# The last modulation group on VectorE inside the down projection, instead of TensorE in the up projection

## The reference, cut to what matters

```python
for l in range(DEPTH_2):
    sh_l, sc_l, g_l = jnp.split(jax.nn.silu(c) @ w_mod[l] + b_mod[l], 3, axis=-1)
    sh_c, sc_c, g_c = jnp.split(jax.nn.silu(c_ctx) @ w_mod[l] + b_mod[l], 3, axis=-1)
    hl = xl * (1.0 + sc_l[:, None, :]) + sh_l[:, None, :]
    hc = xc * (1.0 + sc_c) + sh_c
    ...
```

## Time and profile before

| | us |
|---|---|
| median of three runs | 3048.57 |
| lowest and highest run | 3047.79, 3052.81 |
| the profiled execution | 3046.77 |
| its span, first to last instruction | 3045.0 |
| TensorE busy with matmuls | 2971.8 |
| VectorE busy | 1683.7 |
| ScalarE busy | 1352.8 |
| up projection | about 796 to 1326 |
| down projection | about 1326 to 1574 |

### The profile page before, as it was taken

How to read it: one execution, slowest core, us unless ns; L and a number is a source line. 1 busy time by engine, 2 the same in 40 slices (tenths; PEclk the granted TensorE clock), 3 DMA queues, 4 the chain that set the end, 5 groups by cost and what they waited for, 6 DMA issues and landing times.

```text
span 3045.0 us, 48466 instructions
## 1 busy us (share of the span) xinstructions
PE 2971.8 (98%) x19848; PEld 2526.0 (83%) x19848; DVE 1683.7 (55%) x2625; ACT 1352.8 (44%) x2084; POOL 43.8 (1%) x84
## 2 busy tenths in 40 slices
PE   8999999999899999999999999999999999999997
PEld 7888876898588888788888887788888998889996
DVE  6666666443766666664464325554562575357754
ACT  5333334434455555454452224544442472255543
POOL 1000000000000000000000000000000000000000
PEclk9999999999999999999999999999999999999998
DMA  7665655446765666745553222222232442234442
GB/s 266 223 222 210 220 195 214 140 165 263 276 233 210 228 230 257 279 157 183 185 182 102 97 93 83 76 87 83 83 142 97 166 168 96 97 129 145 153 155 108
DMA packets 73799, 510.03 MB, mean 167 GB/s; under 512 B 8325, under 2 KB 8465, under 8 KB 19601
## 3 DMA queue, kind: packets, MB, share of 16 engines
q1 hardware_dynamic: 63504, 435.74, 40.6%
q0 software_dynamic: 10112, 71.60, 5.9%
HBM read 503.10 MB, written 6.55 MB: 167 GB/s over the span
## 4 chain that ended last, share of the span: by engine, by line
PE 93%; DVE 5%; ACT 1%; DMA 1%; issue 0%; SPq 0%; ACTq 0%; DVEq 0%
PE bank L773 22%; PE bank L717 16%; PE bank L716 8%; PE bank L1496 6%; PE bank L1498 6%; PE bank L1497 6%; PE bank L916 3%; PE bank L917 2%; PE bank L918 2%; PE bank L948 2%; PE bank L1056 2%; PE bank L814 2%; PE bank L815 1%; PE bank L816 1%; PE bank L1123 1%; PE bank L1521 1%
## 5 line engine op out<-in xcount | busy, mean ns | idle before, releaser
L2305 DVE TENSOR_TENSOR ring_f32r<-ring_f,high_f32r 128x1024 fp32r<-128x1024 f32 (+1 forms) x738 | 830.4, 1163 | 718.4 <-ACT high_f32r L1658 697.2
L1658 ACT CAST high_f32r<-ring_f 128x1024 fp32r<-128x1024 f32 (+1 forms) x644 | 609.5, 995 | 821.8 <-PE bank L773 446.6
L717 PE MATMUL bank<-hyz_f32r,high_f32r 128*128 128x512 f32 x2112 | 743.4, 398 | 1.0 <-DVE hyz_f32r L2305 1.0
L716 PE MATMUL bank<-hyz_f32r,ring_f32r 128*128 128x256 f32 x2008 | 562.6, 280 | 3.0 <-DVE hyz_f32r L2305 2.0
L773 PE MATMUL bank<-hyz_f32r,high_f32r 128*128 128x512 f32 (+1 forms) x2016 | 531.8, 341 | 4.3 <-DVE hyz_f32r L2305 2.1
L717 PEld LDWEIGHTS bank<-hyz_f32r,high_f32r 128*128 128x128 f32 x2112 | 391.8, 188 | 101.6 <-issue 15.3
L773 PE MATMUL bank<-hyz_f32r,ring_f32r 128*128 128x512 f32 (+1 forms) x1184 | 411.4, 347 | 0.0
L773 PEld LDWEIGHTS bank<-hyz_f32r,high_f32r 128*128 128x128 f32 x2016 | 349.9, 191 | 48.1 <-issue 2.8
L716 PEld LDWEIGHTS bank<-hyz_f32r,ring_f32r 128*128 128x128 f32 x2008 | 378.9, 189 | 8.5 <-DVE hyz_f32r L2305 2.7
L1496 PE MATMUL bank<-hyz_f32r,high_f32r 128*128 128x512 f32 (+1 forms) x1024 | 359.3, 351 | 3.1 <-DVE ring_f32r L2305 3.1
L1498 PE MATMUL bank<-hyz_f32r,ring_f32r 128*128 128x512 f32 (+1 forms) x1024 | 344.8, 337 | 0.0
(11 more groups left out here) (417 smaller groups left out, 4051.1 us busy)
## 6 DMA issues: line engine op xcount, KB each, us to landing
ring_f<-in_w_in SPq DMA_DIRECT2D x159, 1024.0 KB, 4.9
ring_f<-in_w_up SPq DMA_DIRECT2D x88, 1024.0 KB, 4.9
ring_f<-in_w_out SPq DMA_DIRECT2D x56, 1024.0 KB, 4.9
ring_f<-in_w_mod SPq DMA_DIRECT2D x48, 1024.0 KB, 4.9
ring_f<-in_w_down SPq DMA_DIRECT2D x64, 704.0 KB, 4.1
h_f<-in_w_mod POOLq DMA_DIRECT2D x34, 1024.0 KB, 7.5
ring_f<-in_w_kv SPq DMA_DIRECT2D x8, 1024.0 KB, 5.1
z_f<-in_w_mod POOLq DMA_DIRECT2D x8, 1024.0 KB, 7.9
```

The costliest lines, as they stand in the source:

```text
L716: mm(small, lo, x_hi, start=False, stop=False)
L717: last = mm(bank, hi, pair(x_hi, x_lo), start=start, stop=stop)
L1658: act.copy(w_hi[p % 2][:, half], slot[s % SLOTS][:, half]).then_inc(w_high, 1)
L2305: return v.tensor_tensor(out, in0, in1, op)
```

## The change

The sixteen slabs of group 5 leave the up projection. They are stored the other way round in HBM: 128 outputs on the partitions, the 2048 inputs along the row. In the down projection VectorE multiplies such a slab by the conditioning vector, which lies as the same row on all partitions, and sums along the row, in one instruction with an accumulator output. The slab comes in two halves of 1024 columns, 32 in all, in two buffers; each half is used twice, for `c` and for `c_ctx`. The partial sums of the two halves are added at the end.

To have the conditioning vectors as a row on every partition, they are loaded once more as 32 rows (`c_rows`), put through SiLU by ScalarE, stored to HBM (`c_spread`) by GpSimd, and loaded from there onto all partitions (`c_wide`, 2 MB) at the beginning of the up projection, where the context was loaded before. The context is now loaded behind the last half slab. `mod_c` shrinks from 512 to 64 columns, with overlapping windows of 32. VectorE's loop over the slabs of the down projection is written out.

```diff
-UP_MODS = [4 + 7 * k for k in range(8)] + [62 + 3 * k for k in range(8)]
-UP_TURNED = (29, 61, 85)
+PE_MODS = 80
+UP_MODS = [4 + 7 * k for k in range(8)]
+UP_TURNED = (29, 61)
...
+            def half_slab(h):
+
+                if h >= 2:
+                    pool.wait_ge(S("mod_added"), 2 * h - 2)
+                name, n = (("up_mod_loaded", 448), ("rows_loaded", 112))[h % 2]
+                pool.wait_ge(S(name), n + 16 * (h // 2))
+                load(mod_half[h % 2], d["w_mod"][PE_MODS + h // 2, :, 1024 * (h % 2):1024 * (h % 2) + 1024], name)
+
-            for n in range(NORM_MODS, 48, 2):
+            for n in range(NORM_MODS, 32, 2):
...
                 if n == NORM_MODS:
-                    load(x_all[:, KC * T:], d["ctxT"], "rows_loaded")
+                    load(c_wide, d["c_spread"].to_broadcast([P, 2 * D]), "rows_loaded")
+            pool.wait_ge(gemm_done, TILE0["up"] + 88)
+            pool.wait_ge(S("f_act"), 45)
+            for h in range(32):
+                half_slab(h)
+            pool.wait_ge(S("mod_added"), 64)
+            pool.wait_ge(S("rows_loaded"), 112 + 16 * 16)
+            load(x_all[:, KC * T:], d["ctxT"], "rows_loaded")
...
-                if j == 0:
-                    mod_row_copied(5, 4, up_mod_row)
                 up(84 + j, 0, ("up", 2) if j < 2 else ("down", -86))
-                if j == 3:
-                    mod_copied(5, 5)
...
-            with dve.Fori(0, 7) as i:
-                for k in range(8):
-                    low("down", 4 + k, i)
-                    if k % 4 == 1:
-                        down_added(k // 4, i)
+            def mod_added(n):
+
+                half, s = n // 2, n % 2
+                if n > 1:
+                    dve.wait_ge(S("mod_added"), n - 1)
+                if s == 0:
+                    dve.wait_ge(S(("up_mod_loaded", "rows_loaded")[half % 2]), (448, 112)[half % 2] + 16 * (half // 2 + 1))
+                k = slice(1024 * (half % 2), 1024 * (half % 2) + 1024)
+                v.scalar_tensor_tensor((mod_junk, mod_half[half % 2])[s], mod_half[half % 2], 1.0, c_wide[:, s * D + k.start:s * D + k.stop], ALU.mult, ALU.mult,
+                                       accum_out=mod_part[:, half // 2, 2 * s + half % 2:2 * s + half % 2 + 1]).then_inc(S("mod_added"), 1)
+
+            halves = iter(range(32))
+            for k in range(4, 60):
+                low("down", k)
+                if k % 4 == 1:
+                    down_added(k // 4 - 1)
+                elif k >= 8:
+                    for h in itertools.islice(halves, 1):
+                        mod_added(2 * h)
+                        mod_added(2 * h + 1)
...
-            dve.wait_ge(S("mod_out"), 7)
+            dve.wait_ge(S("mod_out"), 6)
+            dve.wait_ge(S("mod_added"), 64)
+            for s in range(2):
+                step(tt(MOD[:, 80:96, s], mod_part[:, :, 2 * s], mod_part[:, :, 2 * s + 1], ALU.add))
```

More of the change, by code:

```diff
@@ L402, in build @@
         up_sum = [Z[:, FT + n, :] for n in range(4)]
-        mod_c = arena[:, SIZE - 512:SIZE].rearrange("p (k m) -> p k m", m=32)
+        mod_c = arena[:, SIZE - 64:SIZE]
+        mod_part = arena[:, SIZE - 128:SIZE - 64].rearrange("p (n a) -> p n a", a=4)
+        c_rows = arena[0:32, SIZE - 512:SIZE - 384]
+        mod_half = [Y[1][:, 12:16].rearrange("p t n -> p (t n)"), arena[:, SCR.start:SCR.start + 1024]]
+        mod_junk = arena[:, SCR.start + 1024:SCR.start + 2048]
+        c_wide = arena[:, X1_AT:X1_AT + 2 * D]
         mod_row, up_mod_row = kmix, stat
@@ L569, in _ @@
             pool.wait_ge(w_in_slot[1], 16)
+            load(c_rows, d["c_rows"], "mix_loaded")
             load(kmix, d["k_mix"], "mix_loaded")
@@ L584, in _ @@
             pool.wait_ge(S("line_stored"), 32)
+            pool.wait_ge(S("mod_c"), 3)
+            pool.dma_start(d["c_spread"].rearrange("a (p n) -> (a p) n", p=32), c_rows).then_inc(S("line_stored"), 16)
+            pool.wait_ge(S("line_stored"), 48)
             def bias(part):
@@ L933, in _ @@
             pe.wait_ge(loaded, 16)
-            pe.wait_ge(S("mix_loaded"), 16)
+            pe.wait_ge(S("mix_loaded"), 32)
             mm(bk[2][0:A_HEADS, 0:384], vec("table")[0:33, :], kmix[0:33, 0:384], start=True, stop=True
@@ L947, in mod_matvec @@
                 for m in range(4):
-                    last = mm(bk[bank][32 * m:32 * m + 32, :], mod_c[:, n % KC, :], slab[:, m * 512:(m + 1) * 512],
+                    last = mm(bk[bank][32 * m:32 * m + 32, :], mod_c[:, 2 * (n % KC):2 * (n % KC) + 32], slab[:, m * 512:(m + 1) * 512],
                               start=(n % KC == 0), stop=(n % KC == KC - 1))
@@ L1754, in _ @@
             act.wait_ge(S("mod_c"), 1)
-            f(mod_c[:, :, 0:2], vec("c").rearrange("p (k s) -> p k s", s=2), ACT.Silu).then_inc(S("mod_c"), 1)
-            act.wait_ge(S("mod_c"), 2)
+            f(mod_c[:, 0:2 * KC], vec("c"), ACT.Silu).then_inc(S("mod_c"), 1)
+            act.wait_ge(S("mix_loaded"), 32)
+            f(c_rows, c_rows, ACT.Silu).then_inc(S("mod_c"), 1)
+            act.wait_ge(S("mod_c"), 3)
             in1_cast(2)
@@ L2030, in act_high @@
                 if part == 1:
-                    act.wait_ge(S("mod_read"), 96)
+                    act.wait_ge(S("mod_read"), PE_MODS)
                 act.copy(act_hi[part][:, m:m + 4], Z[:, 4 * n:4 * n + 4]).then_inc(S("act_high"), 1)
@@ L2427, in _ @@
                 step(ts(sub, sub, 1.0 - init))
-            dve.wait_ge(S("mix_loaded"), 16)
+            dve.wait_ge(S("mix_loaded"), 32)
             dve.wait_ge(S("sgu_loaded"), 9 * 16)
@@ L2770, in _ @@
                 step(ts(part, part, 1.0, op0=ALU.add))
-            dve.wait_ge(S("rows_loaded"), 112)
+            dve.wait_ge(S("rows_loaded"), 112 + 16 * 17)
             dve.wait_ge(S("down_used"), 3 * 15 + 2)
@@ L3126 @@
         "xT": act(a["x"][0]), "memT": act(a["mem"][0]), "ctxT": act(a["ctx_2"][0]),
-        "w_mod": a["w_mod_2"].reshape(2, 16, P, 3, 4, 4, P).transpose(0, 3, 1, 2, 5, 4, 6).reshape(96, P, D),
+        "w_mod": np.concatenate([
+            a["w_mod_2"].reshape(2, 16, P, 3, 4, 4, P).transpose(0, 3, 1, 2, 5, 4, 6).reshape(96, P, D)[0:PE_MODS],
+            a["w_mod_2"].reshape(2, D, 3, KC, P).transpose(0, 2, 3, 4, 1).reshape(96, P, D)[PE_MODS:]]),
+        "c_rows": np.stack([a["c_2"][0], a["c_ctx_2"]]).reshape(32, P),
         "w_in": tiled(a["w_in"][0], KC)[in1_order()], "w_out": tiled(a["w_out"][0], KC), "w_kv": tiled(a["mem_wkv"][0], KC),
@@ L3146 @@
     d["x_save"] = nc.dram_tensor("x_save", (P, KC * T), F32, kind="Internal").ap()
+    d["c_spread"] = nc.dram_tensor("c_spread", (1, 2 * D), F32, kind="Internal").ap()
     d["out"] = nc.dram_tensor("out_x", (P, KC * T), F32, kind="ExternalOutput").ap()
```

## The result

| | before | after |
|---|---|---|
| median | 3050.45 us (5 runs) | 3033.97 us (5 runs) |
| lowest, highest | 3047.79, 3052.81 | 3033.03, 3036.05 |
| profiled execution, its span | 3046.77, 3045.0 | 3033.97, 3032.2 |

The ratio is 0.9947, with a 95% interval from 0.9934 to 0.9960: 16.5 us less, where 15.4 were forecast, and the median lies 0.8 us over the forecast of 3033.2. On a second occasion the changed kernel had 3034.18 us and the kernel before 3050.02, a difference of 15.8. The forecast had started from 3048.57, the median of three runs; with five runs the median before is 3050.45, 1.9 higher, so that part of its nearness to 3033.97 is luck.

A forecast was written before the change was run, and what follows sets the result against it. TensorE was taken as the bound, holding 93% of the chain that ended last. Terms -16.5 + 0.7 + 0.4 = -15.4 us took the median from 3048.6 to 3033.2 us, range 3029 to 3044.

The forecast's parts named there:

- The up projection, -16.5: Up projection: removing eight insertions of modulation matmuls saves 15.6 us and the last row's turning 0.9, all of it won.
- Rival D: Up projection tiles are paced by something else and stay 6.3 us on average: 3049 us, chance 0.03.
- VectorE in the down projection, +0.7: Down projection: VectorE's and ScalarE's loop of 15.92 us per four slabs slightly exceeds TensorE's 15.80, costing 0.7 us.
- e: Down projection: distance between starts of two new fused VectorE instructions, taken as 1.25 us, with a floor of 1.14.
- the price for the accumulator's read: New VectorE instructions: reading the sum adds to the 1.14 us floor, giving 1.20 to 1.34, taken as 1.25.
- The transfers, 0: Down projection: half slab loads raise traffic to 284 GB/s, under 409, and arrive in time, costing 0 us.
- the landing: Down projection: a half slab lands 4.3 us after issue, like the pooling constants, against 5.1 us until wanted.
- The step's other ground: Down projection: half slabs are issued some 1.4 us behind the ring load, so only part falls together; 0 taken, at most +10 us.
- rival C: Down projection: half slabs come late, past 5.1 us; 3034 to 3043 us, or 3052 at 7 us landing; chance 0.10.
- The context's load: Down projection: moved to about slab 50, it has some 13 slabs (50 us) for the 15 us it took before.
- The end of the stage, +0.4: End of the down projection: two more small VectorE steps of some 0.2 us each before modulating the context.
- The sum, -15.4: Whole kernel: -16.5 + 0.7 + 0.4, from the median 3048.6 to 3033.2 us; 3029.6 for the span; forecast's chance 0.63.

The follow-up runs named there:

- without loads: Changed kernel with all 64 fused instructions but only the first two half slabs loaded, the context's load issued after the last pair; median 3034.97 us.
- the steps early: Changed kernel with the six small modulation steps run in slab 54 instead of behind the last low half; medians 3031.40 and 3031.18 us.
- the dear one with nine: Changed kernel with a third fused instruction of the same size behind each pair, 96 in all; median 3065.3 us.
- one half slab ahead: Changed kernel where a half slab is loaded only when all pairs before it are done; 3107.0 us.

## Why the prediction was right, and where its terms were off

- **The up projection, -16.5.** Measured 541.72 - 525.26 = 16.46, in all traces of the changed form within 0.2. The distance of openings with and without an insertion was the right row to read. Rival D is out.
- **VectorE in the down projection, +0.7.** The term should have been 0. It rested on e = 1.25; e is 1.145, so that the loop (15.3) stays under TensorE (without loads 221.05, as before). The step that failed is the price for the accumulator's read: I took 0.11 us (1.25 against the floor of 1.14), between the 0.06 of VectorE's small instructions and ScalarE's 203 ns, and VectorE's read is hidden to 0.01 us.
- **The transfers, 0.** Measured -0.20, 0.51 and 1.57 us in three traces of the changed kernel, and -0.01 and 1.04 in the two with the steps early, 0.6 on average. The step that failed is the landing: 4.3 us was read from a load that crossed with little beside it; at 262 GB/s the half slabs land after 5.2 to 5.9 us in the median, those of the third pairs after up to 6.9, and the room is 5.1, as forecast. The step's other ground, that only part of a load falls together with a ring load, was not enough either: the ring slabs themselves take 5.6 us in place of 4.1. The sum of the bandwidths fitted, and it wasn't the question. The whole of rival C didn't come, since only one pair in three has so little room, and 0.9 us of a wait is lost in the slack. The context's load, which the forecast gave 50 us of time, was itself in time, but a ring slab came late beside it, and its group was 0.65 us longer in the first trace. In the other two ScalarE waits there too (1.36 and 1.02 us), and TensorE feels nothing.
- **The end of the stage, +0.4.** Measured 0.45.
- **The sum, -15.4.** Over the stretch the three traces have -14.44, -16.21 and -15.44, on average -15.4. That it fits to 0.1 us is luck: +0.7 was forecast for VectorE and 0 for the transfers, and 0 and +0.6 came. The medians say -16.5 and -15.8; the difference lies outside the stretch. Ahead of it one execution of the same kernel stands 10 us behind another, and behind it the changed kernel takes 1473.2 to 1475.4 us; how the medians share this is not shown. For the same cause the step from the profiled execution missed: 3029.6 was forecast for the span and 3032.2 came, 1.2 us of it since the up projection's second tile opened later, 1.0 from a stretch longer than its average; the profiled execution of the kernel before was one with an early opening. In the first trace the two matmuls of the sum of squares behind the tail also took 1.22 us in place of 0.70; why is open.

## What to carry over

An idle share says little about whether work fits: write down the loop through the engines that hand the buffers on, with the distance of starts of each instruction in it, and compare it with the bottleneck's period. Here 8.42 us and 1.145 for each instruction, against 15.8, gave the free case with six and, within 0.1 us a group, the dear one with nine. For transfers compare the landing time under the load of the stretch itself with the room of the tightest buffer, not the mean rate with the limit; where they are equal, a third buffer, laid into memory that is idle then, took the waits out (one trace). And read a gain of a few microseconds from stage borders in the traces when earlier stages vary by more than it.

## What was not expected of the hardware

- VectorE's fused product with a sum along the row, 128x1024 f32 with both tensors from SBUF, takes 1.22 us and the next starts 1.145 us after it; the same without the sum 1.22 and 1.135. The read of the accumulator is a row of 0.08 us, ScalarE's one of 203 ns.
- Transfers of two queues slow each other well below the rate that they reach together: at 262 GB/s a ring slab of 704 KB takes 5.6 us from issue to landing in place of 4.1 (4.0 in the kernel without the loads), and a half slab of 512 KB from GpSimd's queue 5.2 to 5.9, where it took 4.8 to 5.1 at 189 GB/s (one half slab ahead). 409 GB/s were seen in another stretch.
- The opening of the up projection's second tile came between 796.25 and 806.18 us in fourteen traces of kernels that are nearly the same up to there.
